# Squares of q and k: each head's 64 rows folded to 32 on GpSimd, high and low parts in one matmul

## The chip, the cores and the metric

The kernel runs on one core of a Trainium2 chip. The metric is the device time of one execution in microseconds (us). The engines of the core are TensorE (PE, matmuls; PEld is its weight load), VectorE (DVE), ScalarE (ACT), GpSimd (POOL) and SyncE (SP, which issues most of the DMAs). They run side by side, each through its own instructions in order, and meet only at semaphores: an instruction waits until a semaphore has reached a value, and raises another one when it is done.

## The reference

One layer of a hybrid decoder in float32, with x of 1024 tokens by 2048 features. After an RMS norm one projection gives the inputs of three groups of heads: A, 12 heads of dilated window attention; B, 8 heads of forgetting attention; C, 4 heads of gated linear attention. Heads of A and B are 64 wide, and their q and k are normalised by head before the attention:

```python
def rms_norm(x, g):
    xf = x.astype(jnp.float32)
    y = xf * lax.rsqrt(jnp.mean(xf * xf, axis=-1, keepdims=True) + RMS_EPS)
    return (y * g.astype(jnp.float32)).astype(x.dtype)

qa = rms_norm(heads_a(aq), a_q_gain) * scale      # [B, S, heads, 64]
ka = rms_norm(heads_a(ak), a_k_gain)
qb = rms_norm(heads_b(bq), b_q_gain) * scale
kb = rms_norm(heads_b(bk), b_k_gain)
```

The mean of the squares over the 64 features of a head, `jnp.mean(xf * xf)`, is what the change touches. The branch outputs, times a SiLU gate, go through one output projection, and x is added.

## The kernel before, in words

TensorE multiplies float32 values rounded to a shorter form (`fp32r`). To keep the accuracy each operand is split into a high part (rounded by ACT) and a low part (value minus high part, by DVE or POOL), and a product is made of two or three matmuls: high by high, low by high, high by low.

The heads of A and B are worked through in 10 pairs (`PAIRS`), two heads of 64 rows side by side on the 128 partitions: pair 0 (written out), pairs 1 to 4 (a loop), pair 5 (written out), pairs 6 to 8 (a loop), pair 9 (`last_body`). A pair's body does two things at once:

- four groups (`PAIR_GROUPS`) of the input projection, each 8 slots long. In a slot (`half_quarter`) TensorE does 12 matmuls of 512 columns into one of two banks (`acc`, L1805 to L1807). Every second slot needs the next quarter of the weights, rounded by ACT (`split_hi`, `w_hi`, L906) and subtracted by DVE (`split_lo`, `w_lo`, L1325).
- the attention of the pair, and the preparation of the next pair's q and k, as steps between these matmuls. A body has 32 slots (0 to 31). `steps_of(pair, at)` tells which steps stand at which place; `at` is twice the slot for the start of a slot and one more for its middle. Every engine goes through the same list and does its own share of each step, in the order in which `steps_of` gives them: product, turn, scale, score, finish, ..., sum, root, square.

The steps that matter here:

- score(j): PE makes the logits (L1988, L1991), DVE adds the bias and finds the minimum (L1615), ACT takes the exponential (L1191). Two buffers hold the logits, so PE's score(j+1) waits for DVE's of j in the wide ones. scale(j): DVE divides by the sum (L1623, L1625).
- turn(u), product(u): PE transposes the probabilities (L1999), ACT and DVE split them (`pt_hi` L1199, `pt_lo` L1631), PE multiplies them by v (L2014). finish(u): ACT moves half a result to the other partitions (`o_full`, L1210), DVE adds it (L1639).
- square(m), m = 0 to 3 (two halves of 512 tokens of q, then of k) for the next pair: ACT squares 128x512 elements of `raw` twice, into `sq` as float32 (L1148) and into `sq_hi` rounded (L1149); DVE subtracts them into `sq_lo` (L1558). sum(m), one slot later: PE adds the squares over each head's 64 rows by a matmul with a matrix of ones, once for `sq_hi` and once for `sq_lo` (L1960, L1961, into the bank `side`); ACT takes the logarithm of the sum (L1154) and clears the way for the next one. root(i) after two sums: ACT makes x^-1/2 (L1160), DVE scales `raw` by it (L1564). There is one `sq_hi`, so square(m) waits for the semaphore `ssq_done` of sum(m-1).
- low parts: POOL subtracts the high parts of q and k (L880, L883), the only work that it has in the pairs.

The places are numbers: `SLOT_SQUARE = (14, 16, 20, 22)`, sum one slot after, `SLOT_ROOT = (18, 24)`, and for head 1 of a pair `score` 8 and 9 in slot 16, 12 in slot 22, 13 in slot 23. The pairs 1 to 9 get their squares in the bodies of pairs 0 to 8, so each of these steps runs in nine bodies; pair 0 gets its own earlier, in a group before (`FIRST_SQUARE`).

ACT in a group also moves the finished bank to memory (`evac`, `stage`, L950, then two DMA issues in `save`).

Of the kernel before, what the change touches and what calls it, by code (L numbers as in the profile page):

```python
# [20 lines left out]
HALF = 512  # L21
HEAD = 64
# [9 lines left out]
A_PAIRS = A_WIDTH // P  # L32
# [15 lines left out]
C_ALONE = 2 * C_K // P + 2  # L48
HEAD_GROUPS = 3
PAIR_GROUPS = 4  # L50
ITEMS = 2 * NT
# [47 lines left out]
LAST_BOUND, LAST_GATE, LAST_SILU = 15, 16, 18  # L99
SLOT_SQUARE = (14, 16, 20, 22)  # L100
SLOT_ROOT = (18, 24)
# [16 lines left out]
def steps_of(pair, at):  # L118
# [60 lines left out]
def head_columns(c):  # L179

    if isinstance(c, int) and c == 0:
        return COL_CZ, COL_CZ + P, COL_CV + 2 * P
    if isinstance(c, int) and c == 1:
        return COL_CZ + 2 * P, COL_CV + 3 * P, COL_CZ + 3 * P
    return COL_CV + (2 + c) * P, COL_CZ + (2 + c) * P, (c - 2) * A_WIDTH


# [36 lines left out]
def build(nc, x, norm_g, w_in, a_q_gain, a_k_gain, b_q_gain, b_k_gain, fox_bias,  # L224
# [11 lines left out]
    with ExitStack() as ctx:  # L236
# [142 lines left out]
        def early_stage(t):  # L379
# [7 lines left out]

        x_squared, x_logged, x_rooted, x_normed, x_turned, x_hi_done, x_lo_done = (
            sem(n) for n in "x_squared x_logged x_rooted x_normed x_turned x_hi_done x_lo_done".split())
        dist_chain, ws_hi_done, ws_lo_done, small_done, small_out, small_saved, lf_step, c_done = (  # L390
# [5 lines left out]

        q_in, k_in, v_in, z_in, sq_done, sq_lo_done, ssq_done = (
            sem(n) for n in "q_in k_in v_in z_in sq_done sq_lo_done ssq_done ".split())
        normed, qh_done, ql_done, kh_done, k_other_done, kl_done, v_turned, vh_done = (
# [11 lines left out]

        gla_gate, gla_sum, gla_abs, gla_exp, gla_log, gla_min, gla_a, gla_scan = (
            sem(n) for n in "gla_gate gla_sum gla_abs gla_exp gla_log gla_min gla_a gla_scan".split())
        gla_scaled = sem("gla_scaled")
# [383 lines left out]
        def _(pool):  # L798
# [72 lines left out]
            with pool.Fori(1, C_HEADS) as c:  # L871
                gla_head(c)

            def low_parts(pair, h):

# [13 lines left out]
            for h in range(2):  # L889
                low_parts(0, h)  # L890
            with pool.Fori(1, A_PAIRS + B_PAIRS) as p:
                for h in range(2):
                    low_parts(p, h)
# [3 lines left out]
        def _(act):  # L897
# [80 lines left out]
            def row_scale(t):  # L978
                act.wait_ge(x_in[t % X_BUFS], 16 * (t // X_BUFS + 1))
                act.activation(junk[:], x_buf[t % X_BUFS], ACT.Square, accum_out=x_ssq[:, t:t + 1])\  # L980
                    .then_inc(x_squared, 1)

                act.wait_ge(x_squared, t + 1)
                act.activation(x_log[:, t:t + 1], x_ssq[:, t:t + 1], ACT.Ln, scale=1.0 / D_MODEL,
                               bias=eps_col[:]).then_inc(x_logged, 1)
                act.wait_ge(x_logged, t + 1)
                act.activation(x_rstd[:, t:t + 1], x_log[:, t:t + 1], ACT.Exp, scale=-0.5).then_inc(x_rooted, 1)
# [76 lines left out]
            def gla_steps(c, slot):  # L1064
# [3 lines left out]
                if slot == G_GATE:  # L1068
                    act.wait_ge(gla_sum, c + 1)
                    act.activation(g_t[:, 1, :], g_t[:, 0, :], ACT.Abs).then_inc(gla_abs, 1)  # L1070
                    act.wait_ge(gla_abs, c + 1)
                    act.activation(g_t[:, 1, :], g_t[:, 1, :], ACT.Exp, scale=-1.0).then_inc(gla_exp, 1)
                    act.wait_ge(gla_exp, c + 1)
                    act.activation(g_t[:, 1, :], g_t[:, 1, :], ACT.Ln, bias=1.0).then_inc(gla_log, 1)
# [58 lines left out]
            def square(pair, m):  # L1133
# [78 lines left out]
            def steps_at(pair, at, has_next=True):  # L1212
                for name, j in steps_of(pair, at):
# [106 lines left out]
        def _(dve):  # L1320
# [322 lines left out]
            def steps_at(pair, kind, at, next_kind):  # L1643
                for name, j in steps_of(pair, at):
# [23 lines left out]
                    elif name == "root" and next_kind is not None:  # L1668
                        norm(pair + 1, j, next_kind)
                    elif name == "square" and next_kind is not None:  # L1670
# [114 lines left out]
        def _(pe):  # L1785
# [167 lines left out]
            def sum_squares(pair, m):  # L1953
# [187 lines left out]
```

## Time and profile before

| | |
|---|---|
| median of 3 runs | 2126.6 us (2125.61 to 2126.87) |
| the profiled execution | 2125.7 us, span 2124.0 us |
| PE busy | 2072.9 us, 98% of the span |
| DVE busy | 993.4 us, 47% |
| ACT busy | 853.5 us, 40% |
| POOL busy | 246.6 us, 12% |
| mean granted clock of TensorE | 0.994 of full |

The span is the time from the first to the last instruction; 1.7 us lie around it. PE's busy time counts a matmul from its start to its modelled end, and matmuls overlap, so a busy PE says that it had work and not how fast it went. The cadence is read from the starts of matmuls that follow each other. The pairs take the span from about 605 us to 1840 us.

### The profile page before, as it was taken

The page shows a single profiled execution, that of the slowest core. Times are in us where ns is not written, and L with a number is a line of the kernel's source. Part 1 is how long each engine was busy: PE and PEld are TensorE (multiplying, and loading weights), DVE is VectorE, ACT ScalarE, POOL GpSimd, SP SyncE. Part 2 cuts the span into 40 slices and gives each one's busy share as a digit, 9 for nine tenths or more (in the row PEclk, how much of TensorE's full clock was granted, in tenths as well). Part 3 has the DMA queues.
Part 4 walks back from the last instruction along what each step waited for, and adds up shares of the span by engine and source line. Part 5 has one row for each costly group of instructions (what it writes and reads, how often), then busy time and mean ns, then how long its engine had stood idle before and what let it go on. Part 6 is the DMA issues. An engine that isn't in the chain of part 4 may idle for free.

```text
span 2124.0 us, 28699 instructions
## 1 busy us (share of the span) xinstructions
PE 2072.9 (98%) x10376; PEld 1741.5 (82%) x10376; DVE 993.4 (47%) x1571; ACT 853.5 (40%) x1426; POOL 246.6 (12%) x141
## 2 busy tenths in 40 slices
PE   6999999999999999999999999999999988999999
PEld 5788888888878888888888888888888867788887
DVE  6611456474644554545454445455445465512122
ACT  6311243434354445444444445454444454311110
POOL 0000343250520000001010000001010000000000
PEclk9999999999999999999999999999999999999999
DMA  6322323323332222222222222222132363323134
GB/s 222 80 70 69 110 67 105 85 77 107 91 94 64 67 89 74 85 64 69 84 74 84 65 79 85 95 84 92 57 99 84 93 237 117 124 94 127 47 129 148
DMA packets 189769, 201.11 MB, mean 95 GB/s; under 512 B 15992, under 2 KB 138920, under 8 KB 188544
## 3 DMA queue, kind: packets, MB, share of 16 engines
q1 hardware_dynamic: 172976, 169.70, 27.0%
q10 hardware_dynamic: 16720, 30.45, 3.8%
q8 instruction: 44, 0.72, 0.1%
q14 instruction: 29, 0.24, 0.0%
HBM read 151.33 MB, written 48.78 MB: 94 GB/s over the span
## 4 chain that ended last, share of the span: by engine, by line
PE 83%; DVE 6%; ACT 4%; DMA 3%; issue 3%; SPq 1%; ACTq 0%; DVEq 0%
PE acc L1805 18%; PE acc L1807 17%; PE acc L1806 17%; PE pv L2014 4%; PE turned L1999 4%; PE scores L1991 2%; PE scores L1988 2%; DMA w_raw<-in_w_in_dram 1%; PE pv L1895 1%; PE scores L2104 1%; PE side L1895 1%; PE scores L2105 1%; PE turned L2105 1%; PE acc L2105 1%; PE scores L2106 1%
## 5 line engine op out<-in xcount | busy, mean ns | idle before, releaser
L1805 PE MATMUL acc<-act_hi,w_hi 128*128 128x512 f32 x1856 | 743.1, 400 | 8.8 <-DVE w_lo L1325 3.3
L1807 PE MATMUL acc<-act_hi,w_lo 128*128 128x512 f32 x1856 | 725.8, 391 | 0.0
L1806 PE MATMUL acc<-act_lo,w_hi 128*128 128x512 f32 x1856 | 724.2, 390 | 0.0
L1805 PEld LDWEIGHTS acc<-act_hi,w_hi 128*128 128x128 f32 x1856 | 349.5, 188 | 78.6 <-DVE w_lo L1325 6.9
L1807 PEld LDWEIGHTS acc<-act_hi,w_lo 128*128 128x128 f32 x1856 | 348.8, 188 | 76.0
L1806 PEld LDWEIGHTS acc<-act_lo,w_hi 128*128 128x128 f32 x1856 | 349.6, 188 | 65.1
L1325 DVE TENSOR_TENSOR w_lo<-w_raw,w_hi 128x512 fp32r<-128x512 f32 x223 | 206.2, 925 | 315.1 <-ACT w_hi L906 315.1
L1631 DVE TENSOR_TENSOR pt_lo<-turned,pt_hi 128x1024 fp32r<-128x1024 f32 (+1 forms) x120 | 114.9, 958 | 253.1 <-ACT pt_hi L1199 252.1
L1191 ACT ACTIVATE prob<-prob,neg_max 128x128 f32<-128x128 f32 (+7 forms) x160 | 124.1, 776 | 251.8 <-DVE neg_max L1615 251.8
L1199 ACT ACTIVATE pt_hi<-turned 128x1024 fp32r<-128x1024 f32 (+1 forms) x120 | 97.5, 812 | 242.0 <-PE turned L1999 242.0
L906 ACT ACTIVATE w_hi<-w_raw 128x512 fp32r<-128x512 f32 x223 | 139.2, 624 | 132.1 <-PE acc L1807 107.3
L880 POOL TENSOR_TENSOR q_st<-raw,q_st 64x1024 fp32r<-64x1024 f32 x20 | 49.5, 2475 | 993.9 <-ACT q_st L1168 993.9
L1615 DVE CUSTOM_DVE_ANT_0 prob<-scores,logit_bias 128x128 f32<-128x128 f32 (+7 forms) x160 | 118.3, 753 | 40.4 <-PE scores L1991 38.8
L1737 DVE TENSOR_TENSOR w_lo<-w_raw,w_hi 128x512 fp32r<-128x512 f32 x49 | 33.9, 693 | 213.7 <-ACT w_hi L930 213.7
L930 ACT ACTIVATE w_hi<-w_raw 128x512 fp32r<-128x512 f32 x49 | 31.0, 632 | 229.4 <-PE side L2106 209.4
L950 ACT ACTIVATE stage<-acc 128x512 f32<-128x512 f32 x112 | 66.7, 595 | 121.5 <-PE acc L1807 121.4
L1999 PE MATMUL turned<-ident,prob 128*128 128x128 f32 x720 | 98.5, 273 | 0.4 <-DVE prob L1625 0.3
L2014 PE MATMUL pv<-pt_lo,v_st 128*128 128x256 f32 (+1 forms) x400 | 94.2, 290 | 0.0
L1999 PEld LDWEIGHTS turned<-ident,prob 128*128 128x128 f32 x720 | 83.7, 140 | 12.9 <-DVE prob L1625 2.3
L2014 PE MATMUL pv<-pt_hi,v_st 128*128 128x256 f32 (+1 forms) x400 | 87.6, 269 | 0.4 <-DVE pt_lo L1631 0.4
L1988 PE MATMUL scores<-k_hi,q_st 128*128 128x512 f32 (+1 forms) x240 | 82.8, 347 | 3.9 <-DVE neg_max L1615 2.7
L1625 DVE TENSOR_SCALAR prob<-prob,inv_denom 128x128 f32<-128x128 f32 (+7 forms) x160 | 83.3, 520 | 5.7
(291 smaller groups left out, 2767.4 us busy)
## 6 DMA issues: line engine op xcount, KB each, us to landing
w_raw<-in_w_in_dram SPq DMA_DIRECT2D x240, 256.0 KB, 2.8
proj_scratch<-stage ACTq DMA_DIRECT2D x116, 256.0 KB, 2.1
w_raw<-in_w_out_dram SPq DMA_DIRECT2D x71, 256.0 KB, 3.0
raw<-proj_scratch SPq DMA_DIRECT2D x20, 512.0 KB, 3.2
act_lo<-mixed_scratch SPq DMA_DIRECT2D x7, 1024.0 KB, 6.8
res<-in_x_dram SPq DMA_DIRECT2D x24, 256.0 KB, 5.3
out_dram<-res SPq DMA_DIRECT2D x24, 256.0 KB, 2.9
extra_raw<-in_w_out_dram SPq DMA_DIRECT2D x23, 256.0 KB, 3.2
```

The source lines that it names most:

```text
L906: act.activation(w_hi[:, slot, :], w_raw[:, slot, :], ACT.Copy).then_inc(hi_done, 1)
L1191: act.activation(prob[:, j % 2, 0:n], prob[:, j % 2, 0:n], ACT.Exp, scale=-1.0, bias=neg_max[:, j:j + 1], accum_out=denom[:, j:j + 1]).the ...
L1199: act.activation(pt_hi[:, 0:n], turned[:, 0:n], ACT.Copy).then_inc(pth_done, 1)
L1325: dve.tensor_tensor(w_lo[:, slot, :], w_raw[:, slot, :], w_hi[:, slot, :].bitcast(F32), ALU.subtract)\
L1615: dve.tensor_tensor_reduce(out=prob[:, j % 2, 0:n], in0=scores[:, c0:c0 + n], in1=bias, scale=1.0, scalar=3e38, op0=ALU.add, op1=ALU.min, ...
L1631: dve.tensor_tensor(pt_lo[:, 0:n], turned[:, 0:n], pt_hi[:, 0:n].bitcast(F32), ALU.subtract)\
L1805: pe.matmul(acc, hi, xh, start=first, stop=False)
L1806: pe.matmul(acc, hi, xl, start=False, stop=False)
L1807: mm = pe.matmul(acc, lo, xh, start=False, stop=end)
L1988: pe.matmul(scores[:, o + c0:o + c1], q, k_hi[:, h, c0:c1], start=True, stop=False)
L1999: mm = pe.transpose(turned[:, o:o + P], prob[:, q, c * P:(c + 1) * P], ident[:])
L2014: mm = pe.matmul(pv[:, (2 * (d % 2) + q) * P:(2 * (d % 2) + 2) * P], v_st[:, h, c, :], (pt_hi, pt_lo)[part][:, o:o + (2 - q) * P], start=( ...
```

## The change

For pair 0 nothing is changed. For the nine other pairs:

- square(m): ACT squares `raw` once, into `sq` (float32).
- fold, new, on POOL: the squares of the last 32 rows of each head are made again from `raw` into `vz` (two 32x512 products), and added to `sq` (128x512). The first 32 rows of each head in `sq` then hold sums of two squares.
- round, new, on ACT: `sq` is rounded into `sq_hi`.
- DVE writes the low parts of the folded rows beside the high ones, into the last 32 rows of each head of `sq_hi` (two 32x512 subtractions in place of one 128x512).
- sum(m): one matmul over `sq_hi` in place of two.

The places are new: squares in slots 13, 15, 19 and 21, round two slots after the square, sum three slots after. The roots stay in slots 18 and 24. DVE's share of the square goes from the place of "square" to that of "round". square(m) keeps its wait for `ssq_done` of sum(m-1). Some semaphores of the first stages are merged into one (`x_chain`, `gla_soft`), which orders the same instructions.

```diff
-SLOT_SQUARE = (14, 16, 20, 22)
+SLOT_SQUARE = (13, 15, 19, 21)
...
-    out += [("sum", m) for m in range(4) if SLOT_SQUARE[m] + 1 == slot]
+    out += [("sum", m) for m in range(4) if SLOT_SQUARE[m] + 3 == slot]
+    out += [("round", m) for m in range(4) if SLOT_SQUARE[m] + 2 == slot]
     out += [("root", i) for i in range(2) if SLOT_ROOT[i] == slot]
     out += [("square", m) for m in range(4) if SLOT_SQUARE[m] == slot]
...
+            def fold(pair, m):
+
+                pool.wait_ge(sq_done, squared(pair, m))
+                moved = 1 + 12 * (pair - 1) + 3 * m
+                at = slice((m % 2) * HALF, (m % 2 + 1) * HALF)
+                if m == 0:
+                    pool.wait_ge(ql_done, 2 * pair)
+                    pool.wait_ge(kl_done, 2 * pair)
+                pool.wait_ge(sq_folded, moved)
+                for h in range(2):
+                    near, far = (slice(h * HEAD + r, h * HEAD + r + FOLD) for r in (0, FOLD))
+                    pool.tensor_tensor(vz[near, HALF:], raw[far, m // 2, at], raw[far, m // 2, at], ALU.mult)\
+                        .then_inc(sq_folded, 1)
+                pool.wait_ge(sq_folded, moved + 2)
+                pool.tensor_tensor(sq[:, m % 2, :], sq[:, m % 2, :], vz[:, HALF:], ALU.add)\
+                    .then_inc(sq_folded, 1)
...
                 act.activation(sq[:, m % 2, :], src, ACT.Square).then_inc(sq_done, 1)
-                act.activation(sq_hi[:], src, ACT.Square).then_inc(sq_done, 1)
+                if first_pair(pair):
+                    act.activation(sq_hi[:], src, ACT.Square).then_inc(sq_rounded, 1)
+
+            def round_folded(pair, m):
+
+                act.wait_ge(sq_folded, 1 + 12 * (pair - 1) + 3 * m + 3)
+                act.wait_ge(ssq_done, 4 * pair + m)
+                act.activation(sq_hi[:], sq[:, m % 2, :], ACT.Copy).then_inc(sq_rounded, 1)
...
             def square(pair, m):
-                dve.wait_ge(sq_done, 2 * (4 * pair + m + 1))
-                dve.tensor_tensor(sq_lo[:, m % 2, :], sq[:, m % 2, :], sq_hi[:].bitcast(F32),
-                                  ALU.subtract).then_inc(sq_lo_done, 1)
+                dve.wait_ge(sq_done, squared(pair, m))
+                dve.wait_ge(sq_rounded, 4 * pair + m + 1)
...
+                    for h in range(2):
+                        near, far = (slice(h * HEAD + r, h * HEAD + r + FOLD) for r in (0, FOLD))
+                        dve.tensor_tensor(sq_hi[far, :], sq[near, m % 2, :], sq_hi[near, :].bitcast(F32),
+                                          ALU.subtract).then_inc(sq_lo_done, 1)
...
-                pe.wait_ge(sq_lo_done, 4 * pair + m + 1)
-                pe.matmul(side[:], half_ones_r[:], sq_hi[:], start=True, stop=False)
-                pe.matmul(side[:], half_ones_r[:], sq_lo[:, m % 2, :], start=False, stop=True).then_inc(ssq_done, 1)
+                else:
+                    pe.wait_ge(sq_lo_done, 4 + 8 * (pair - 1) + 2 * m + 2)
+                    mm = pe.matmul(side[:], half_ones_r[:], sq_hi[:], start=True, stop=True)
+                mm.then_inc(ssq_done, 1)
```

How the instructions stand. First ACT, slots 21 to 23 of a body before the change (`pt_hi` belongs to turn 7, the exponentials of 640 and 768 columns to scores 12 and 13, `sq<-side` is the logarithm of a sum, `stage` the move of a bank):

```order
L1154 ACTIVATE sq<-side,eps_col 128x512 [waits ssq_done]
L1199 ACTIVATE pt_hi<-turned 128x896 [waits t_done,pv_done]
L1191 ACTIVATE prob,denom<-prob,neg_max 128x640 [waits masked]
L1148 ACTIVATE sq<-raw 128x512 [waits ssq_done,normed]
L1149 ACTIVATE sq_hi<-raw 128x512
L906 ACTIVATE w_hi<-w_raw 128x512 [waits w_landed0,quarter_done]
L950 ACTIVATE stage<-acc 128x512 [waits proj_saved0,half_done]
L1191 ACTIVATE prob,denom<-prob,neg_max 128x768 [waits masked]
L1210 ACTIVATE o_full<-pv 64x512 [waits pv_done]
L1154 ACTIVATE sq<-side,eps_col 128x512 [waits ssq_done]
```

The same slots after the change:

```order
L1190 ACTIVATE sq_hi<-sq 128x512 [waits ssq_done,sq_folded]
L1182 ACTIVATE sq<-raw 128x512 [waits ssq_done,normed]
L1240 ACTIVATE pt_hi<-turned 128x896 [waits t_done,pv_done]
L1232 ACTIVATE prob,denom<-prob,neg_max 128x640 [waits masked]
L1195 ACTIVATE sq<-side,eps_col 128x512 [waits ssq_done]
L940 ACTIVATE w_hi<-w_raw 128x512 [waits w_landed0,quarter_done]
L984 ACTIVATE stage<-acc 128x512 [waits proj_saved0,half_done]
L1232 ACTIVATE prob,denom<-prob,neg_max 128x768 [waits masked]
L1251 ACTIVATE o_full<-pv 64x512 [waits pv_done]
L1190 ACTIVATE sq_hi<-sq 128x512 [waits ssq_done,sq_folded]
```

Square 3 has moved from behind the exponential of score 12 to ahead of `pt_hi`. The instruction that makes `sq_hi` for sum 3 was ahead of the exponential of score 13 and stands behind it and behind `o_full` now.

DVE in slots 22 and 23 before the change, behind score 12, through score 13 (768 columns) and what follows:

```order
L1558 TENSOR_TENSOR sq_lo<-sq,sq_hi 128x512 [waits sq_done]
L1325 TENSOR_TENSOR w_lo<-w_raw,w_hi 128x512 [waits hi_done]
L1623 RECIPROCAL inv_denom<-denom 128x1 [waits exp_done]
L1625 TENSOR_SCALAR prob<-prob,inv_denom 128x640 [waits recip_done]
L1613 REGISTER_ALU [waits s_done]
L1615 ISA prob,neg_max<-scores,logit_bias 128x768
L1615 ISA neg_max 128x1
L1639 TENSOR_TENSOR o_full<-pv,o_full 64x512 [waits o_moved]
```

And after it:

```order
L1368 TENSOR_TENSOR w_lo<-w_raw,w_hi 128x512 [waits hi_done]
L1673 RECIPROCAL inv_denom<-denom 128x1 [waits exp_done]
L1675 TENSOR_SCALAR prob<-prob,inv_denom 128x640 [waits recip_done]
L1663 REGISTER_ALU [waits s_done]
L1665 ISA prob,neg_max<-scores,logit_bias 128x768
L1665 ISA neg_max 128x1
L1689 TENSOR_TENSOR o_full<-pv,o_full 64x512 [waits o_moved]
L1608 TENSOR_TENSOR sq_hi<-sq,sq_hi 32x512 [waits sq_rounded,sq_done]
L1608 TENSOR_TENSOR sq_hi<-sq,sq_hi 32x512
```

The low part for sum 3 stood right behind score 12; its two instructions stand behind score 13 and the sum of `o_full` now. On PE sum 3 moves from the start of slot 23 (behind score 13) to the start of slot 24, behind the 12 projection matmuls of slot 23.

## Rows read from the trace of the kernel before

**Rows 1.** The page: busy time, share of the span and instructions of each engine
```profile
PE 2072.9 (98%) x10376; PEld 1741.5 (82%) x10376; DVE 993.4 (47%) x1571; ACT 853.5 (40%) x1426; POOL 246.6 (12%) x141
```

**Rows 2.** Waits of PE, 640 to 1640 us: total, times, longest (us)
```profile
PE scores L1988 <- DVE neg_max L1615: 2.5, 8, 0.4
```

**Rows 3.** Timeline of PE, a body: start, duration (us), instruction
```profile
822.79 0.40 PE L1960 MATMUL side<-sq_hi,half_ones_r 128*128 128x512 f32 x1
...
823.26 0.39 PE L1805 MATMUL acc<-act_hi,w_hi 128*128 128x512 f32 x1
```

**Rows 4.** The same, slot 23
```profile
830.19 0.34 PE L2014 MATMUL pv<-pt_hi,v_st 128*128 128x256 f32 x2
...
831.12 0.40 PE L1988 MATMUL scores<-k_hi,q_st 128*128 128x512 f32 x1
...
832.29 0.39 PE L1805 MATMUL acc<-act_hi,w_hi 128*128 128x512 f32 x1
...
835.01 0.39 PE L1805 MATMUL acc<-act_hi,w_hi 128*128 128x512 f32 x1
```

**Rows 5.** Timeline of ACT, slots 21 to 23 of that body
```profile
825.59 0.92 ACT L1199 ACTIVATE pt_hi<-turned 128x896 fp32r<-128x896 f32 x1 [1.44 <-PE turned L1999]
...
828.61 0.83 ACT L1191 ACTIVATE prob<-prob,neg_max 128x640 f32<-128x640 f32 x1 [2.10 <-DVE neg_max L1615]
...
833.47 0.94 ACT L1191 ACTIVATE prob<-prob,neg_max 128x768 f32<-128x768 f32 x1 [1.90 <-DVE neg_max L1615]
...
834.53 0.59 ACT L1210 ACTIVATE o_full<-pv 64x512 f32<-64x512 f32 x1
```

**Rows 6.** Timeline of DVE, the same slots
```profile
826.54 1.09 DVE L1631 TENSOR_TENSOR pt_lo<-turned,pt_hi 128x896 fp32r<-128x896 f32 x1 [4.91 <-ACT pt_hi L1199]
827.74 0.82 DVE L1615 CUSTOM_DVE_ANT_0 prob<-scores,logit_bias 128x640 f32<-128x640 f32 x1
...
831.21 0.69 DVE L1325 TENSOR_TENSOR w_lo<-w_raw,w_hi 128x512 fp32r<-128x512 f32 x1
...
832.48 0.95 DVE L1615 CUSTOM_DVE_ANT_0 prob<-scores,logit_bias 128x768 f32<-128x768 f32 x1
```

**Rows 7.** The tile sq_lo, all pairs: min/median/max ns, first and last start
```profile
L1558 DVE TENSOR_TENSOR sq_lo<-sq,sq_hi x40: 691/693/694, 609.0 to 1657.1; 128x512 fp32r<-128x512 f32 x40
```

**Rows 8.** Timeline of DVE and ACT, slots 15 to 17 of that body
```profile
805.18 1.09 DVE L1631 TENSOR_TENSOR pt_lo<-turned,pt_hi 128x896 fp32r<-128x896 f32 x1 [3.60 <-ACT pt_hi L1199]
806.18 0.28 DVE L1615 CUSTOM_DVE_ANT_0 prob<-scores,logit_bias 128x128 f32<-128x128 f32 x1
...
809.50 0.69 DVE L1325 TENSOR_TENSOR w_lo<-w_raw,w_hi 128x512 fp32r<-128x512 f32 x1
...
810.95 0.68 DVE L1639 TENSOR_TENSOR o_full<-pv,o_full 64x512 f32<-64x512 f32 x1
```
**Rows 9.** ACT there
```profile
807.72 0.62 ACT L1148 ACTIVATE sq<-raw 128x512 f32<-128x512 f32 x1
```

**Rows 10.** Groups of POOL by shape: busy us, mean ns | idle before
```profile
L855 POOL TENSOR_TENSOR q_level<-g_qk,g_t 96x512 f32<-96x512 f32 x28 | 47.6, 1701 | 133.4 <-ACT g_t L1078 133.3
```

**Rows 11.** Timeline of POOL, then of DVE, where both work
```profile
844.34 2.55 POOL L880 TENSOR_TENSOR q_st<-raw,q_st 64x1024 fp32r<-64x1024 f32 x1 [83.44 <-ACT q_st L1168]
...
845.76 1.68 DVE L1325 TENSOR_TENSOR w_lo<-w_raw,w_hi 128x512 fp32r<-128x512 f32 x1 [1.13 <-ACT w_hi L906]
```

**Rows 12.** Timeline of PE, its two first long waits in the last body (in brackets)
```profile
1730.60 0.50 PE L2063 MATMUL acc<-w_hi,act_hi 128*128 128x512 f32 x1 [3.23 <-DVE w_lo L1730]
...
1749.35 0.80 PE L2063 MATMUL acc<-extra_hi,act_hi 128*128 128x512 f32 x1 [3.30 <-DVE extra_lo L1730]
```

**Rows 13.** Windows: length, busy us of PE, PEld, DVE, ACT, POOL, granted clock, DMA
```profile
837.00:953.00 116.00, 115.68 (x595) 97.82 (x595) 57.56 (x107) 55.12 (x94) 10.43 (x4) 1.00 0.25 75
...
1731.00:1735.00 4.00, 4.00 (x12) 3.13 (x11) 3.89 (x7) 1.77 (x3) 0.00 (x0) 0.57 0.19 66
...
1749.30:1755.30 6.00, 5.95 (x14) 4.70 (x15) 3.39 (x5) 2.65 (x5) 0.00 (x0) 0.50 0.69 261
```

More of the change, by code:

```diff
@@ L49 @@
 HEAD_GROUPS = 3
+FOLD = 32
 PAIR_GROUPS = 4
@@ L185, in head_columns, with squared @@
     return COL_CV + (2 + c) * P, COL_CZ + (2 + c) * P, (c - 2) * A_WIDTH
+def squared(pair, m):
+    return 4 * pair + m + 1
 def first_head(c):
@@ L395, in build @@
             sem(n) for n in "hi_done lo_done quarter_done half_done evac_done".split())
-        q_in, k_in, v_in, z_in, sq_done, sq_lo_done, ssq_done = (
-            sem(n) for n in "q_in k_in v_in z_in sq_done sq_lo_done ssq_done ".split())
+        q_in, k_in, v_in, z_in, sq_done, sq_folded, sq_rounded, sq_lo_done, ssq_done = (
+            sem(n) for n in "q_in k_in v_in z_in sq_done sq_folded sq_rounded sq_lo_done ssq_done ".split())
         normed, qh_done, ql_done, kh_done, k_other_done, kl_done, v_turned, vh_done = (
@@ L410, in build @@
             sem(n) for n in "gla_rank_in gla_up_in gla_bias_in gla_q_in gla_k_in gla_v_in gla_z_in gla_saved".split())
-        gla_gate, gla_sum, gla_abs, gla_exp, gla_log, gla_min, gla_a, gla_scan = (
-            sem(n) for n in "gla_gate gla_sum gla_abs gla_exp gla_log gla_min gla_a gla_scan".split())
+        gla_gate, gla_sum, gla_soft, gla_log, gla_min, gla_a, gla_scan = (
+            sem(n) for n in "gla_gate gla_sum gla_soft gla_log gla_min gla_a gla_scan".split())
         gla_scaled = sem("gla_scaled")
@@ L890, in _ @@
                 low_parts(0, h)
-            with pool.Fori(1, A_PAIRS + B_PAIRS) as p:
+            pool.wait_ge(ql_done, 2)
+            pool.wait_ge(kl_done, 2)
+            pool.memset(vz[:, HALF:], 0.0).then_inc(sq_folded, 1)
+            for m in range(4):
+                fold(1, m)
+            pool.wait_ge(sq_folded, 13)
+            for h in range(2):
+                low_parts(1, h)
+            with pool.Fori(2, PAIRS) as p:
+                for m in range(4):
+                    fold(p, m)
+                pool.wait_ge(sq_folded, 12 * p + 1)
                 for h in range(2):
@@ L1069, in gla_steps @@
                     act.wait_ge(gla_sum, c + 1)
[L1070 to L1073, printed above, removed]
+                    act.activation(g_t[:, 1, :], g_t[:, 0, :], ACT.Abs).then_inc(gla_soft, 1)
+                    act.wait_ge(gla_soft, 2 * c + 1)
+                    act.activation(g_t[:, 1, :], g_t[:, 1, :], ACT.Exp, scale=-1.0).then_inc(gla_soft, 1)
+                    act.wait_ge(gla_soft, 2 * c + 2)
                     act.activation(g_t[:, 1, :], g_t[:, 1, :], ACT.Ln, bias=1.0).then_inc(gla_log, 1)
@@ L1229, in steps_at @@
                         square(pair + 1, j)
+                    elif name == "round" and has_next:
+                        round_folded(pair + 1, j)
                     elif name == "sum" and has_next:
@@ L1556, in square @@
             def square(pair, m):
-                dve.wait_ge(sq_done, 2 * (4 * pair + m + 1))
-                dve.tensor_tensor(sq_lo[:, m % 2, :], sq[:, m % 2, :], sq_hi[:].bitcast(F32),
-                                  ALU.subtract).then_inc(sq_lo_done, 1)
+                dve.wait_ge(sq_done, squared(pair, m))
+                dve.wait_ge(sq_rounded, 4 * pair + m + 1)
+                if first_pair(pair):
+                    dve.tensor_tensor(sq_lo[:, m % 2, :], sq[:, m % 2, :], sq_hi[:].bitcast(F32),
+                                      ALU.subtract).then_inc(sq_lo_done, 1)
+                else:
+                    for h in range(2):
+                        near, far = (slice(h * HEAD + r, h * HEAD + r + FOLD) for r in (0, FOLD))
+                        dve.tensor_tensor(sq_hi[far, :], sq[near, m % 2, :], sq_hi[near, :].bitcast(F32),
+                                          ALU.subtract).then_inc(sq_lo_done, 1)
             def norm(pair, i, kind):
@@ L1669, in steps_at @@
                         norm(pair + 1, j, next_kind)
-                    elif name == "square" and next_kind is not None:
+                    elif name == "round" and next_kind is not None:
                         square(pair + 1, j)
@@ L1958, in sum_squares @@
                     pe.wait_ge(vl_done, 2 * pair)
-                pe.wait_ge(sq_lo_done, 4 * pair + m + 1)
-                pe.matmul(side[:], half_ones_r[:], sq_hi[:], start=True, stop=False)
-                pe.matmul(side[:], half_ones_r[:], sq_lo[:, m % 2, :], start=False, stop=True).then_inc(ssq_done, 1)
+                if first_pair(pair):
+                    pe.wait_ge(sq_lo_done, m + 1)
+                    pe.matmul(side[:], half_ones_r[:], sq_hi[:], start=True, stop=False)
+                    mm = pe.matmul(side[:], half_ones_r[:], sq_lo[:, m % 2, :], start=False, stop=True)
+                else:
+                    pe.wait_ge(sq_lo_done, 4 + 8 * (pair - 1) + 2 * m + 2)
+                    mm = pe.matmul(side[:], half_ones_r[:], sq_hi[:], start=True, stop=True)
+                mm.then_inc(ssq_done, 1)
             def values(pair, b):
```

12 lines of the change are left out of this document (6 added, 6 removed).

## The prediction

> **What bounds the kernel now.** I read the page first: PE is busy for 98% of the span, every other engine for less than half [rows 1]. Then PE's waits over 1000 us of the pairs: there is one kind, for DVE's minimum of the logits, 2.5 us in all [rows 2]. The window of one body (116 us) shows PE busy for 115.68 us at a clock of 1.00 [rows 13]. So in the pairs PE is the bound, with every other engine just in time. A matmul less is worth its cadence there; a wait of PE, wherever it comes from, is paid in full, because nothing later has slack to give it back.
>
> **What is removed.** Sum(m) loses one of two matmuls. The two start 0.47 us before the next projection matmul [rows 3], so one costs 0.235 us. Four per body, nine bodies: 36 x 0.235 = 8.5 us. That is the whole gain. ACT does as many instructions as before (a rounding for a second squaring). DVE's subtraction of 0.69 us [rows 7] becomes two; 32 rows instead of 128 don't shorten it if time goes by the 512 columns, as in the row of 64 x 512 elements that takes 0.68 us [rows 8]. So DVE gets 4 x 0.6 = 2.4 us more per body, in an engine busy for half of it.
>
> **What is added on POOL.** Three instructions of 512 columns per fold. The trace has 1.70 us for 96x512 [rows 10] and 2.55 us for 1024 columns, 1.28 us for half of it [rows 11]. I take 1.28, nearer in kind (contiguous), and keep 1.70 as the upper end: a fold takes 3.8 to 5.1 us. POOL had nothing there. Its own time matters only where ACT waits for it: fold 1 is over, by the chain below, 4.5 to 5.8 us after sum 0, and ACT comes to round 1 at 5.9. Covered at both ends, barely at the upper one.
>
> **What is moved.** This decides. Square(m) still waits on ACT for sum(m-1). Before, the sum stood one slot after its square and ahead of the next one. Now square 1 stands in slot 15 on ACT while sum 0 stands in slot 16 on PE, and square 3 in slot 21 while sum 2 stands in slot 22. ACT stops at these two squares until PE gets there, and with it what is queued behind: `pt_hi`, then on DVE `pt_lo`, the minimum, and so on. The piece of ACT's and DVE's order in the section on the change shows the second worse part: what makes the operand of sum 3 now stands behind everything that score 13 needs, and score 13 is issued by PE only one half-quarter ahead of sum 3.
>
> *Place two, sum 2 to sum 3.* I count from S, the landing of sum 2. The chain is serial: square 3 on ACT 0.6 [rows 9]; `pt_hi` to `pt_lo` 0.95 (825.59 to 826.54 [rows 5, 6]); `pt_lo` to the minimum of score 12 1.0 (as 805.18 to 806.18 [rows 8]); to its exponential 0.87 (827.74 to 828.61); that exponential 0.83 [rows 5]; logarithm of sum 2 and `w_hi`, of the same 128x512 as the square, 2 x 0.6; `w_lo` to the minimum of score 13 1.27 (831.21 to 832.48 [rows 6]); to its exponential 0.99 (to 833.47); to `o_full` 1.06 (to 834.53); `o_full` and the rounding 2 x 0.6; the two subtractions 1.3; hand-over to PE 0.1. Sum: S + 11.4. PE meanwhile: the next matmul starts 0.16 before S (0.39 long, 0.23 apart), 12 matmuls 2.72 (832.29 to 835.01), product 0.93 (830.19 to 831.12), score 13 0.70 (831.12 to 832.29 less 0.47 for the two sums), 12 matmuls 2.72 [rows 4]: ready at S + 6.9. PE waits 4.5 us; 0.1 of it falls at product 7, which waits for `pt_lo`, and the rest in one piece at sum 3.
>
> *Place one, sum 0 to sum 1.* From the landing of sum 0: square 1 0.6, `pt_hi` 0.95, `pt_lo` 1.0, from the minimum of score 8 to the end of exponential 9 1.54 (806.18 to 807.72 [rows 8, 9]), logarithm and `w_hi` 1.2, `w_lo` through two scalings 1.45 (809.50 to 810.95), the addition of `o_full` 0.6, two subtractions 1.3, hand-over 0.1: 8.75. PE: -0.16 + 2.72 + 0.93 + 2.72 + 0.3 for three transposes = 6.5. It waits 2.2 us, in pieces (product 5, turn 6, sum 1).
>
> Sums 0 and 2 themselves have cover: their folds and roundings run while nothing is held. In the body before, PE waits at none of these places [rows 2], so the 6.7 us are new.
>
> **The clock.** After a wait of PE of 3.23 us the granted clock is 0.57 over the next 4 us, and after one of 3.30 us it is 0.50 over 6 us [rows 12, 13], that is the level of 1.2 GHz instead of 2.4. The first costs 0.43 x 4 = 1.7 us, the second 0.50 x 6 = 3.0. I take 1.7, since what surrounds it there (PE busy throughout after the wait) is like a body, and keep 3.0 as the upper end. The wait at sum 3 is longer than both, so I expect the fall in each body. It comes where PE is the only bound again, and is paid. The Trainium skill, "TensorE: Matmul & The Clock Gate", section "HAM oscillation — how this bites in real kernels", says in general that long idle gaps of PE put its clock down and that the matmuls behind them pay; the trace agrees with the numbers just given.
>
> **The sum.** Per body: -0.94 + 4.5 + 2.2 + 1.7 = +7.46 us. Nine bodies: +67.1. On the profiled execution's 2125.7 that gives 2192.8; the median of the runs is 0.9 above it. I take 2193.
>
> **A second page that speaks against the change.** While POOL worked from 844.34 to 846.89, DVE's `w_lo`, which takes 0.69 us elsewhere, took 1.68 and ended 0.55 after POOL's instruction [rows 11]. New POOL work of 4 x 3.8 us per body puts `w_lo`, scalings and the subtractions at that risk: each can be late by up to one POOL instruction, 1.3 us. The Trainium skill, "SBUF — State Buffer", section "🔬 SBUF: two separate sides", says that the two engines share one port pair, which one instruction holds to its end while the other is blocked; the trace agrees (1.68 beside 0.69).
>
> **The rivals.**
> 1. *The clock does not fall.* Everything else as above: 9 x 5.8 = +52, 2178 us. For it: those falls were seen in the last body, where PE had been idle more often just before. Against it: two of two waits of that size.
> 2. *POOL is slow and in the way.* Instructions of 1.70 us, so that round 1 or sum 2 waits some 0.6 us, and DVE is blocked once or twice on the way to sums 1 and 2 for 0.6 us each: +1.8 per body, 2193 + 16 = 2209 us.
> 3. *Only the last link counts.* If ACT is not really held at the squares (PE reaches the sums before ACT wants them), what is left is the part from score 13 on: 0.99 + 1.06 + 1.2 + 1.3 + 0.1 + 0.2 for the end of the score = 4.85 against 2.72 of cover, 2.1 us per body, too short for the clock: 9 x (2.1 - 0.94) = +10.5, 2136 us. Against it: ACT idles 1.4 to 2.1 us just ahead of these places [rows 5], so it is there before PE.
> 4. *The other side: the cover holds.* Between a square and its sum lie at least two slots of 3.6 us (a body of 116 us has 32), 7.2 us; the fold's 3.8 us, a rounding and two subtractions make 5.8. Were ACT and DVE free at round 3, nothing would wait and the 8.5 us would be kept: 2118 us. It decides at sum 3: true if DVE's subtractions end within 2.7 us of score 13's end. Against it: the order of the instructions, which puts 4.85 us of work there.
>
> **How the numbers follow.** Forecast 0.52, rival 1 0.20, rival 2 0.12, rival 3 0.10, rival 4 0.06. The range should hold the forecast with its upper clock price (3.0 instead of 1.7: +12, 2205), rival 1 with waits a fifth smaller (9 x 4.4 = +40, 2166) and rival 2; it goes from 2155 to 2212 and leaves out rivals 3 and 4. A difference of 0.2%, 4.3 us, is about what a measurement of this kernel can tell from none. Faster 0.05 (rival 4), within it 0.02 (rival 3 shrunk to the size of the gain), slower 0.93.
>
> **What would show it.** In the profile after: PE's waits get a row for the sum's `side` matmul, released by DVE's subtraction, of 30 to 45 us in total with a longest near 4.4; nine granted-clock dips right behind; `pt_hi` after the square of slots 15 and 21 delayed, with ACT's squares waiting for PE's `side`; a body of 122 to 125 us. POOL's new instructions near 1.3 us. It would be wrong if sum 3 waits under 1 us, or if a body is as long as before.

## The result, and the profile after

The changed kernel is slower: 2196.99 us (2192.46 to 2197.79, 5 runs) beside 2126.43 us (2125.01 to 2126.87, 5 runs), a ratio of 1.0328 with a 95% interval of 1.0314 to 1.0342. The forecast was 2193. The profiled execution took 2194.7 us with a span of 2193.0, 69.0 more than before. Where spans or waits are compared, one profiled execution stands for each kernel; the runs of one kernel differ by up to 8 us.

The first line of the page answers to [rows 1]. PE has 36 matmuls less and is busy for longer, and its share has fallen; POOL has 128 us more work:

```profile
PE 2090.8 (95%) x10340; PEld 1745.1 (80%) x10340; DVE 1028.4 (47%) x1607; ACT 854.1 (39%) x1426; POOL 374.7 (17%) x250
```

PE's waits from 640 to 1740 us (total, times, longest) answer to [rows 2]. The one kind that was there is as small as before; the new one is the sum's matmul, held by DVE's subtraction, twice in each of nine bodies:

```profile
PE side L2015 <- DVE sq_hi L1608: 51.3, 18, 4.4
PE scores L2043 <- DVE neg_max L1665: 2.8, 8, 0.4
```

The same body as in [rows 4], on PE (start, duration, idle before in brackets): product 7, score 13, the projection's matmuls of slot 23, and then nothing until 846.69. The matmul that follows sum 3 lasts 0.63 us instead of 0.39:

```profile
837.81 0.45 PE L2069 MATMUL pv<-pt_hi,v_st 128*128 128x256 f32 x2
...
838.85 0.40 PE L2043 MATMUL scores<-k_hi,q_st 128*128 128x512 f32 x1
...
841.60 0.39 PE L1855 MATMUL acc<-act_hi,w_hi 128*128 128x512 f32 x1
...
846.69 0.79 PE L2015 MATMUL side<-sq_hi,half_ones_r 128*128 128x512 f32 x1 [4.25 <-DVE sq_hi L1608]
847.28 0.63 PE L1855 MATMUL acc<-act_hi,w_hi 128*128 128x512 f32 x1
```

ACT in these slots, to be read beside [rows 5]. It stands idle for 3.11 us until PE's sum 2 releases square 3; only then come `pt_hi`, the exponential, the logarithm, `w_hi`, the next exponential, `o_full`, and last the rounding for sum 3. Over all nine bodies (640 to 1740 us) ACT waits 65.6 us for `side` at its squares, 18 times; its row (total, times, longest) stands first, then the timeline of the body:

```profile
ACT sq L1182 <- PE side L2015: 65.6, 18, 4.2
```

```profile
835.19 0.63 ACT L1182 ACTIVATE sq<-raw 128x512 f32<-128x512 f32 x1 [3.11 <-PE side L2015]
835.72 0.90 ACT L1240 ACTIVATE pt_hi<-turned 128x896 fp32r<-128x896 f32 x1
838.52 0.83 ACT L1232 ACTIVATE prob<-prob,neg_max 128x640 f32<-128x640 f32 x1 [1.90 <-DVE neg_max L1665]
...
839.35 0.67 ACT L1195 ACTIVATE sq<-side,eps_col 128x512 f32<-128x512 f32 x1
839.92 0.62 ACT L940 ACTIVATE w_hi<-w_raw 128x512 fp32r<-128x512 f32 x1
...
842.84 0.93 ACT L1232 ACTIVATE prob<-prob,neg_max 128x768 f32<-128x768 f32 x1 [1.81 <-DVE neg_max L1665]
...
843.89 0.59 ACT L1251 ACTIVATE o_full<-pv 64x512 f32<-64x512 f32 x1
844.50 0.63 ACT L1190 ACTIVATE sq_hi<-sq 128x512 fp32r<-128x512 f32 x1
```

DVE, beside [rows 6]: the two subtractions are a pair of 1.40 us behind all of it, and end 0.05 us before PE starts:

```profile
840.57 0.69 DVE L1368 TENSOR_TENSOR w_lo<-w_raw,w_hi 128x512 fp32r<-128x512 f32 x1 [2.08 <-ACT w_hi L940]
...
841.84 0.95 DVE L1665 CUSTOM_DVE_ANT_0 prob<-scores,logit_bias 128x768 f32<-128x768 f32 x1
...
844.51 0.70 DVE L1689 TENSOR_TENSOR o_full<-pv,o_full 64x512 f32<-64x512 f32 x1 [1.71 <-ACT o_full L1251]
845.24 1.40 DVE L1608 TENSOR_TENSOR sq_hi<-sq,sq_hi 32x512 fp32r<-32x512 f32 x2
```

The windows (length, busy us of PE, PEld, DVE, ACT, POOL, granted clock, DMA) answer to [rows 13]: over 124 us, almost a whole body, the clock is 0.97, and over the 7 us at the end of the wait and behind it 0.51, which is the lower level of 1.2 GHz:

```profile
800.00:924.00 124.00, 117.89 (x590) 98.46 (x589) 61.47 (x111) 56.14 (x95) 24.52 (x16) 0.97 0.24 72
845.00:852.00 7.00, 5.31 (x13) 4.21 (x14) 4.24 (x7) 2.88 (x5) 0.00 (x0) 0.51 0.10 37
```

Read in windows of half a microsecond from 640 to 1740 us, the clock falls nine times, once a body, and PE's busy time there times the missing part of the clock sums to 18.6 us (1.7 us before, in one fall of the last body).

**Where the 69 us are.** Waits at the sums 51.3; clock 18.6 - 1.7 = 16.9; removed matmuls -7.7 (the span in e6); together 60.5. The 8.5 us left are 0.9 us a body. The profile counts a wait only from the modelled end of the matmul before, which lies 0.16 us behind the time at which the next could have started: 2.9 us over 18 waits. PE's weight loads wait 6.0 us for `pt_lo` (18 times, at products 5 and 7) and 4.7 us for the scaled probabilities (13 times), 10.7 together, where the same two rows of the kernel before have 3.1. The 7.6 us more are an upper bound, since a weight load can wait beside matmuls that still run. The two terms are large enough for what is left; how it divides between them is not shown.

### The profile page after: what moved, and what is told of

Same layout as the page of the kernel before. It is cut to its first block, busy times and chain, and to the rows that moved or that the text cites. A ratio compares the mean times of both kernels' runs of the same rounds, so it can differ in the third digit from the quotient of the medians.

```text
span 2193.0 us, 29005 instructions
## 1 busy us (share of the span) xinstructions
PE 2090.8 (95%) x10340; PEld 1745.1 (80%) x10340; DVE 1028.4 (47%) x1607; ACT 854.1 (39%) x1426; POOL 374.7 (17%) x250
## 4 chain that ended last, share of the span: by engine, by line
PE 76%; DVE 9%; ACT 6%; issue 5%; DMA 3%; SPq 1%; ACTq 1%; DVEq 0%
PE acc L1855 16%; PE acc L1857 16%; PE acc L1856 15%; PE turned L2054 3%; PE pv L2069 3%; PE scores L2046 2%; DVE prob L1665 2%; PE scores L2043 2%; DVE w_lo L1368 1%; PE pv L1945 1%; DMA w_raw<-in_w_in_dram 1%; DVE sq_hi L1608 1%; PE scores L2159 1%; PE side L1945 1%; PE scores L2160 1%
## 5 line engine op out<-in xcount | busy, mean ns | idle before, releaser
L1368 DVE TENSOR_TENSOR w_lo<-w_raw,w_hi 128x512 fp32r<-128x512 f32 x223 | 216.8, 973 | 365.1 <-ACT w_hi L940 365.1
L891 POOL TENSOR_TENSOR vz<-raw 32x512 f32<-32x512 f32 x72 | 76.4, 1061 | 525.3 <-ACT sq L1182 522.6
L1787 DVE TENSOR_TENSOR w_lo<-w_raw,w_hi 128x512 fp32r<-128x512 f32 x49 | 33.9, 693 | 213.6 <-ACT w_hi L964 213.6
```

The source lines that it names most:

```text
L1368: dve.tensor_tensor(w_lo[:, slot, :], w_raw[:, slot, :], w_hi[:, slot, :].bitcast(F32), ALU.subtract)\
```

## The experiments

Each ratio is taken against runs of the kernel before on the same chip; their medians were 2125.5 us for e1 to e4, 2127.06 for e5 to e8 and 2126.44 for e9 and e10. The changed kernel's runs stand beside a fourth set (2126.43), than which it is 70.6 us slower. So a difference of 1 or 2 us between the medians of two experiments says nothing.

### e1: no wait of the squares for the sums

```diff
-                if m > 0:
+                if m > 0 and first_pair(pair):
                     act.wait_ge(ssq_done, 4 * pair + m)
```

> The changed kernel, with one wait less: for pairs 1 to 9 the square of step m no longer waits on ScalarE for the sum of step m-1 (sq_hi, which that wait once guarded, is now written by the rounding, and that keeps its own wait). Theory (both waits of TensorE start at ScalarE being held at squares 1 and 3, and the part from score 13 on adds its own 2 us): the wait at sum 1 (1.4 us a body) goes, the wait at sum 3 falls from 4.3 to about 2.4 us, about 31 us less from the waits in nine bodies, less if the clock still falls after a wait of 2.4 us: 2160 to 2170 us. Rival A (ScalarE is not really held there, the place of the rounding behind score 13 does it all): no change, 2195 us. Rival B (GpSimd's folds set the time): no change at sum 1 either, 2195 us.

2147.0 us (2142.56 to 2150.93), ratio 1.0094 [1.0071, 1.0116]: 50 us of the 70 are gone, more than the theory gave. PE's waits:

```profile
PE side L2015 <- DVE sq_hi L1608: 21.2, 9, 2.4
PE scores L2043 <- DVE neg_max L1665: 3.1, 9, 0.4
```

The wait at sum 1 is gone and that at sum 3 is 2.3 to 2.4 us, as the chain had it. What I had left out is that the clock then falls in 6 of 9 bodies instead of 9 (9.9 us in place of 18.6), and that with the held squares the small waits at products 5 and 7 go and those at turn 6 shrink. The profiled execution is the slowest of the four (2150.93 us, granted clock 0.990; the others have 0.991 to 0.994), so the others lost less to the clock than these 9.9 us. Both rivals, which gave no change, are out: ACT is really held there, and this one wait, which guards nothing in the new kernel (the rounding has its own for `sq_hi`), makes most of the loss.

### e2: the rounding at the front of its place

```diff
-    out += [("round", m) for m in range(4) if SLOT_SQUARE[m] + 2 == slot]
...
-    out = [("values", b) for b in range(2) if ...]
+    out = [("round", m) for m in range(4) if SLOT_SQUARE[m] + 2 == slot]
+    out += [("values", b) for b in range(2) if ...]
```

> The changed kernel, with the rounding and the two subtractions moved to the front of their place in the order (ahead of the exponential of score 13 and of o_full in slot 23, ahead of scale and finish in slot 17); the wait of the squares for the sums is kept. Theory (two causes in series): sum 3 no longer stands behind score 13, so its wait falls from 4.3 to about 1 us, but ScalarE now stops for the fold ahead of the exponential, so some waiting moves to the transposes of turns 6 and 8, about 1.5 us each: 2160 to 2170 us. Rival A (the order behind score 13 is all there is): 2197 minus 9 x (4.3 + clock 2.4) = 2137 us or less. Rival B (held squares are all there is): no change, 2195 us.

2168.97 us (2168.11 to 2171.45), ratio 1.0208 [1.0188, 1.0228], inside the theory's range. PE's waits show the waiting moved, in pieces of at most 1.7 us:

```profile
PE turned L2054 <- DVE prob L1675: 28.8, 18, 1.7
PE pv L2069 <- DVE pt_lo L1681: 6.5, 9, 0.8
PE side L2015 <- DVE sq_hi L1608: 5.7, 9, 0.8
```

The sum of these three is 41.0, only 10 less than in the changed kernel, and yet the span is 27 us shorter: the clock does not fall once from 640 to 1740 us, where it cost the changed kernel 18.6 us.

The number came as expected, the reason for the moved waits did not. ACT waits for the fold nine times here (26.4 us) and did so nine times in the changed kernel (24.4 us); in the body from 800 to 850 us it is round 2 in both, and at rounds 1 and 3 ACT does not stop. What is late is DVE: its two subtractions stand ahead of a scaling and of the next minimum now. The rows are shown at e3, where the same order has no held squares beside it.

### e3: both edits

> Both edits together: no wait of the squares for the sums, rounding at the front of its place. Theory: the two causes are additive in part; TensorE waits about 1.9 us a body in pieces too short for the clock to fall: 2130 to 2140 us. Rival (a third cause, GpSimd's work itself or DVE's 2.4 us more a body): stays above 2150 us. A result under 2120 us would say that the waits at products and turns that I expect from the fold ahead of the exponential do not come.

2133.62 us (2132.95 to 2135.93), ratio 1.0039 [1.0027, 1.0052]. PE waits 6.8 us at products and 5.0 at turns, none at the sums. There is no third cause of any size. It is still slower than before, but not because ACT stops for the fold, as I had expected: ACT comes to round 3 straight from its last instruction (830.56 below, with no idle time before it). DVE's pair of subtractions takes 1.40 us ahead of the scaling and the minimum of score 13, which starts 3.18 us after `w_lo` where it was 1.27 in [rows 6]; PE then waits 0.72 us at the transposes that need the scaled result of score 13 (at 837.66), and 0.8 at the product behind. The rows of DVE, with ACT's rounding among them:

```profile
830.21 0.69 DVE L1368 TENSOR_TENSOR w_lo<-w_raw,w_hi 128x512 fp32r<-128x512 f32 x1 [2.08 <-ACT w_hi L940]
830.56 0.63 ACT L1190 ACTIVATE sq_hi<-sq 128x512 fp32r<-128x512 f32 x1
831.29 1.40 DVE L1608 TENSOR_TENSOR sq_hi<-sq,sq_hi 32x512 fp32r<-32x512 f32 x2 [0.39 <-ACT sq_hi L1190]
833.39 0.95 DVE L1665 CUSTOM_DVE_ANT_0 prob<-scores,logit_bias 128x768 f32<-128x768 f32 x1
```

### e4: matmuls that nobody reads, inside the wait

```diff
                 else:
+                    if m == 3:
+                        for f in range(12):
+                            pe.matmul(side[:], half_ones_r[:], act_hi[:, f, 0:HALF], start=True, stop=True)
                     pe.wait_ge(sq_lo_done, 4 + 8 * (pair - 1) + 2 * m + 2)
```

> The changed kernel, with 12 matmuls of 512 columns that nobody reads put ahead of sum 3's wait (they write the bank that sum 3 overwrites). They fill 2.8 us of the 4.3 us wait. Theory (the clock falls because of the long wait and costs about 2.4 us a body): TensorE stays at the full clock, the end of the wait does not move, and 9 x 2.4 = 21 us come back: 2172 to 2180 us. Rival (the fall of the clock costs nothing because something else is late behind it anyway, or it falls in spite of the filling): 2195 us. If the 12 matmuls delayed the sum, it would be slower than 2197 us.

2179.08 us (2178.33 to 2180.36), ratio 1.025 [1.0231, 1.027]: 108 matmuls more and 17.9 us less than the changed kernel. In the timeline the filling stands in the wait, and sum 3 starts 7.84 us after score 13 (846.29 less 838.45), as in the changed kernel (846.69 less 838.85):

```profile
838.45 0.40 PE L2046 MATMUL scores<-k_hi,q_st 128*128 128x512 f32 x1
...
841.88 2.88 PE L2016 MATMUL side<-act_hi,half_ones_r 128*128 128x512 f32 x12
846.29 0.50 PE L2018 MATMUL side<-sq_hi,half_ones_r 128*128 128x512 f32 x1 [1.53 <-DVE sq_hi L1608]
```

The window from 640 to 1740 us, with the same columns as above, has the clock at 1.00, where it was 0.98:

```profile
640.00:1740.00 1100.00, 1070.03 (x5453) 895.84 (x5452) 552.81 (x1001) 496.07 (x841) 219.11 (x144) 1.00 0.24 75
```

That prices the clock at 17 to 18 us by a second way, 1.8 to 2.0 a body (17.9 by the medians, 16.6 by the two ratios).

### e5: the new places and waits without the fold

ScalarE's rounding waits for the square alone, POOL's fold is gone, DVE subtracts once, PE does two matmuls:

```diff
-                act.wait_ge(sq_folded, 1 + 12 * (pair - 1) + 3 * m + 3)
+                act.wait_ge(sq_done, 4 * pair + m + 1)
...
-                for m in range(4):
-                    fold(p, m)
```

> The changed kernel's places and waits (squares in slots 13, 15, 19, 21, rounding two slots later, sum three slots later, square m waiting for sum m-1), but without the fold: GpSimd does nothing new, ScalarE rounds the squares, DVE subtracts once over 128 rows, and TensorE does the two matmuls as before. Theory (places and waits make the whole loss): the same waits of TensorE at sums 1 and 3, a bit shorter by one subtraction (0.6 us each), the clock still falls, and the 8.5 us of the removed matmuls are lost again: 2190 to 2200 us. Rival (the fold on GpSimd makes the loss, by its time or by the port that it shares with DVE): near the kernel before, 2127 to 2140 us.

2185.85 us (2181.91 to 2189.96), ratio 1.0279 [1.0261, 1.0296]. The lower end of the theory's range is missed by 4 us, and the rival is far off: places and waits alone lose 59 us, with GpSimd doing nothing new. The two waits are 0.8 us shorter each on average, 0.7 at sum 3, which is the length of the missing second subtraction:

```profile
PE side L2004 <- DVE sq_lo L1596: 37.5, 18, 3.6
```

e5 still has the 36 matmuls, so the changed kernel's loss without its gain is 70.6 + 7.7 = 78.3 us, of which 59 are in e5. The 19 us between them are the 13.8 us by which the waits are shorter and the clock, which falls in 7 of 9 bodies here (13.4 us in place of 18.6). The second subtraction accounts for most of it; little is left for POOL's work itself. In two bodies a wait of 3.54 and one of 3.41 us brought no fall.

### e6: the kernel before with one matmul in the sums

```diff
-                pe.matmul(side[:], half_ones_r[:], sq_hi[:], start=True, stop=False)
-                pe.matmul(side[:], half_ones_r[:], sq_lo[:, m % 2, :], start=False, stop=True).then_inc(ssq_done, 1)
+                if first_pair(pair):
+                    pe.matmul(side[:], half_ones_r[:], sq_hi[:], start=True, stop=False)
+                mm = pe.matmul(side[:], half_ones_r[:], sq_lo[:, m % 2, :] if first_pair(pair) else sq_hi[:],
+                               start=not first_pair(pair), stop=True)
```

> The kernel before, in which the sums of pairs 1 to 9 leave out the matmul over the low parts (36 matmuls of 512 columns less); everything else stands as it was. It leaves out the low parts' share of the sum of squares. Theory (TensorE is the bound in the pairs): 36 x 0.235 = 8.5 us less, 2118 us. Rival (a matmul of this kind is hidden behind other waits): 2126 us.

2119.38 us (2117.18 to 2121.62), ratio 0.9965 [0.9952, 0.9979]; the span is 2116.3, 7.7 less than before. The gain that the change is after is there, within the interval in full: 8.5 was the estimate.

### e7: other places, in half slots, and no wait for the sums

```diff
-SLOT_SQUARE = (13, 15, 19, 21)
-SLOT_ROOT = (18, 24)
+AT_SQUARE = (22, 24, 37, 41)
+AT_ROUND = (27, 29, 40, 44)
+AT_SUM = (30, 33, 44, 48)
+AT_ROOT = (35, 50)
...
+                if m > 0 and first_pair(pair):
                     act.wait_ge(ssq_done, 4 * pair + m)
```

> The changed kernel with other places, in half slots: squares at 22, 24, 37, 41, roundings at 27, 29, 40, 44, sums at 30, 33, 44, 48, roots at 35, 50 (the changed kernel: 26, 30, 38, 42; 30, 34, 42, 46; 32, 36, 44, 48; 36, 48), and without the squares' wait for the sums. No rounding stands behind the exponential of score 13 in the same place any more, and the fold has 4 to 5 half slots. Theory (the fold is sound, only its places and the old wait lost the time): TensorE waits at no sum and keeps the gain of the matmuls, 2116 to 2119 us. Rival (GpSimd's added work costs DVE time on the port that they share): 2125 to 2135 us.

2119.85 us (2116.96 to 2121.91), ratio 0.9969 [0.9957, 0.9981]: 0.9 us above the theory's range, faster than both kernels (7 us less than before), and as fast as e6, which leaves the low parts out. The rival is out. No sum is among PE's waits from 640 to 1740 us any more:

```profile
PE scores L2045 <- DVE neg_max L1667: 3.1, 9, 0.4
PE turned L2056 <- DVE prob L1677: 0.2, 1, 0.2
```

POOL does as much here as in the changed kernel and DVE too, so their meetings cost the kernel nothing that I can see, though DVE's `w_lo` has a mean of 946 ns where e9 has 921. Two things were changed at once here, the places and the wait; the new places with the old wait were not run. A square and its sum lie 3.5 to 4.5 slots apart now, where the changed kernel has 3.

### e8: GpSimd's products made twice

```diff
+                    pool.tensor_tensor(vz[far, HALF:], raw[far, m // 2, at], raw[far, m // 2, at], ALU.mult)\
+                        .then_inc(sq_folded, 1)
                     pool.tensor_tensor(vz[near, HALF:], raw[far, m // 2, at], raw[far, m // 2, at], ALU.mult)\
                         .then_inc(sq_folded, 1)
```

> The changed kernel with each of GpSimd's two products made twice (the second result is not used): a fold takes 5.4 us in place of 3.4. Theory (round 2 and round 1 become late on ScalarE, since a fold is then longer than its slack of 1 to 2.5 us; the rest waits as before): TensorE waits about 3 us a body more, 2215 to 2230 us. Rival (GpSimd's time has no part in the loss at all): 2197 us.

2229.64 us (2226.44 to 2230.28), ratio 1.0479 [1.0463, 1.0495]. The fold was close to its bound: 2.1 us more of it bring 32.7 us (3.6 a body), more waits at sums (61.2 us, 26 times) and at turns (8.0), and ACT's roundings wait for the fold 26 times (62.6 us), where it was 9 times (24.4). The rival is out: GpSimd's time had cover in the changed kernel, but only about 1 us of it. There fold 1 ended 1.1 us before ACT came to its rounding (816.48 and 817.58), and DVE's subtractions for sum 2, behind a rounding that did wait for its fold, ended 1.1 us before PE started the sum (833.57 and 834.70).

The clock took part too: it falls 13 times from 640 to 1740 us, 26.9 us in place of 18.6. Five of these falls come at sum 1, where PE waits 1.47 us as in the changed kernel, but now with a wait of 0.87 us just ahead and 0.55 us of transposes between them:

```profile
823.24 0.55 PE L2056 MATMUL turned<-ident,prob 128*128 128x128 f32 x3 [0.87 <-DVE prob L1677]
825.25 0.79 PE L2017 MATMUL side<-sq_hi,half_ones_r 128*128 128x512 f32 x1 [1.47 <-DVE sq_hi L1610]
825.84 0.63 PE L1857 MATMUL acc<-act_hi,w_hi 128*128 128x512 f32 x1
```

### e9: the places of e7 with two matmuls and no fold

> The new places of e7 (squares at 22, 24, 37, 41, roundings at 27, 29, 40, 44, sums at 30, 33, 44, 48, roots at 35, 50, no wait of the squares for the sums) without the fold: GpSimd does nothing new and TensorE does two matmuls a sum. Theory (what e7 gains is the removed matmuls, 36 x 0.235 = 8.5 us, and nothing is hidden in the places): 2125 to 2128 us, the same as the kernel before. Rival (the new places themselves are better than those of before, and the fold adds nothing): 2119 us, as e7.

2124.85 us (2122.51 to 2126.64), ratio 0.9994 [0.9985, 1.0003]: no difference from before. The places gain nothing by themselves, and the merged semaphores, which this kernel has too, cost nothing that can be seen. From e9 to e7 the ratio falls by 0.0025, 5 us, and the span by 7.8 (2123.0 to 2115.2); the estimate of 8.5 for the matmuls is at or above the upper end of what the intervals leave, and whether the fold takes some of it back stays open.

### e10: e1 with eight matmuls inside the wait

> e1 (the changed kernel without the squares' wait for the sums) with 8 matmuls that nobody reads ahead of sum 3's wait; they fill 1.8 us of its wait of 2.4 us. In e1 the granted clock fell in 6 of 9 bodies behind that wait, at a price of 9.9 us. Theory (the fall comes from the wait, also at 2.4 us): no fall, 2134 to 2141 us. Rival (it comes from something else in the body): 2147 us.

2141.16 us (2140.35 to 2141.78), ratio 1.0071 [1.0056, 1.0087], 5.8 less than e1 and 0.2 above the theory's range. The intervals of the two ratios overlap, so the times alone don't separate e10 from e1; the clock does. It falls in none of the nine bodies, and all four runs have a mean of 0.996 or 0.997 where e1's have 0.990 to 0.994. So the falls in e1 came from a wait of 2.4 us.

## Why the prediction was right

**The gain.** 36 x 0.235 = 8.5 us against 7.7 of the span and 7.7 of the medians in e6. Right, within the interval.

**POOL.** The products over 32 rows took 1.04 us at the median (1061 ns mean) and the addition over 128 rows 1.30 at the median (1429 ns mean), 3.4 us a fold and 3.8 where `w_lo` meets it (2.14 + 1.62 at 827.57), at or under my lower end of 3.8. That they have cover was right, and e8 shows how little: rival 2 was nearer than its price of 16 us suggests.

**The chain from sum 2 to sum 3.** I counted 11.4 us from the landing of sum 2. Sum 2 starts at 834.70 and lasts 0.45, sum 3 starts at 846.69: 11.54. PE was to wait 4.4 us in one piece; it waits 4.25 in the body shown, and 0.16 more if one counts from when the next matmul could have started. The reason why the chain could be added up from rows of the kernel before is that its instructions are the same, only queued behind each other, and that nothing in it has slack.

**The chain from sum 0 to sum 1.** 8.75 us counted, 8.58 measured (811.75 + 0.39 to 820.72). Less the 6.5 counted for PE's own work that is 2.1 us of waiting where 2.2 were counted; 1.47 of it stand in one piece, the rest in small ones. Both chains begin with ACT held by PE, which e1 showed by taking the wait away, and e2 and e3 showed the second link, the place of the rounding.

**The clock.** 1.7 us a body expected, 2.1 measured (18.6 in nine), 1.8 to 2.0 by e4. The rival in which the clock does not fall is out. The price was between my two rows (1.7 and 3.0). That the fall comes in every body was right, but my reason for it was thin: two falls behind two waits of 3.2 and 3.3 us. In e5, behind nine waits of 3.4 to 3.6 us, it came seven times.

**The sum.** 7.46 us a body predicted. A body took 125.9 us (sum 3 of two bodies seven apart, 846.69 and 1728.24) where it took 118.1 before (831.82 and 1658.40): 7.9. I had called a body 116 us by the length of the window that I read; that window is shorter than a body. The error touched rival 4, whose cover it would have made larger, and the sign of a body of 122 to 125 us, which the measured 125.9 misses.

**The signs.** One more missed: the row for the sum's matmul was to hold 30 to 45 us and holds 51.3. The longest, 4.4, was right. By the prediction's own chains the row should have been larger: 9 x 4.4 = 40 at sum 3 alone, to which most of 9 x 2.2 at sum 1 comes. Measured are 38.0 and 13.3. The sum itself used the full waits, so the forecast does not suffer from it.

**The rivals.** Rival 3, only the last link, is what is left in e1: 2.3 to 2.4 us of wait a body where I had counted 2.1, and 2147 instead of 2136 us, because I had called the wait too short for the clock; it was not, in 6 of 9 bodies. Rival 4 is right in one thing: room enough between square and sum keeps the gain, as e7 shows, though with 3.5 to 4.5 slots; in e3, with the 3 slots of the change, 8 us of loss remain.

**The two rules cited.** Nine long waits brought nine falls of the clock, and none came when the wait was filled (e4, e10) or cut up (e2); in e8 two short waits close together brought five. The rule on idle gaps in the Trainium skill's page "TensorE: Matmul & The Clock Gate" (section "HAM oscillation — how this bites in real kernels") is borne out in that direction. `w_lo` took 1.56 us in slot 20, beside the fold, instead of 0.69, which agrees with the exclusive port of the Trainium skill's page "SBUF — State Buffer" (section "🔬 SBUF: two separate sides"). In e7 such meetings happen too, though milder ones (`w_lo` took 1.18 us at 790.91, beside a product of the fold), and PE waits for none of them, so they have cover there.

## What to carry to other kernels

When a step is split and spread over engines, go through every wait of the old version and ask what it still guards: here one that guarded `sq_hi` was left on the instruction that no longer writes it, and with the new places it made an engine that runs in order stop for PE, 30 us of waits and most of 50. Where an instruction stands among its neighbours matters as much as its slot: the operand for the next matmul must not be made behind the answer to the last one (the changed kernel), nor just ahead of what the next answer needs (e2, e3). And a long wait of TensorE costs more than its length, by a third to a half here (16.9 on 51.3 us in the changed kernel, 9.9 on 21.2 in e1), while four fifths of the same waiting in pieces of up to 1.7 us, well apart, did not (e2).

## What the runs showed of the hardware that I had not expected

- The clock fell behind single waits of PE of 4.1 to 4.4 us nine times of nine (the changed kernel), of 3.4 to 3.6 us seven of nine (e5), of 2.3 to 2.4 us six of nine (e1), and of 1.5 to 1.7 us not at all (e2, 18 of them). The length alone does not decide it: in e1 the three waits of 2.26 us all brought a fall, and waits of 2.39 and 2.40 us did not. And two waits of 0.87 and 1.47 us with 0.55 us of work between them brought it five times of nine (e8).
- In the body shown the clock had fallen by 845.0, while PE was still waiting (from 842.4 to 846.7), and rose again at about 851.8, 5 us after the matmuls began.
- On POOL a product over 32 rows takes 1.04 us and an addition over 128 rows 1.30 for the same 512 columns; the product reads one tile twice, the addition two, so rows or operands may make the difference. On DVE 32 rows take 0.68 us and 128 rows 0.69.
